# Two feed-forwards of a float32 transformer kernel: chunks 1 and 2 as seven block products instead of eight

## The reference

```python
def swiglu(x, w_gate, w_up, w_down):
    return (jax.nn.silu(x @ w_gate) * (x @ w_up)) @ w_down

x = x + 0.5 * swiglu(rmsnorm(x, g_ffn1[l]), w1_gate[l], w1_up[l], w1_down[l])
...
x = x + 0.5 * swiglu(rmsnorm(x, g_ffn2[l]), w2_gate[l], w2_up[l], w2_down[l])
```

## Time and profile before

| | |
|---|---|
| median of 3 executions | 2512.41 us (2511.56 to 2513.01) |
| profiled execution | 2513.3 us, of it the span from first to last instruction 2511.5 us |
| PE busy | 2466.2 us, 98% of the span |
| DVE busy | 1601.0 us, 64% |
| ACT, POOL busy | 892.9 us (36%), 385.6 us (15%) |
| chain that ended last | 87% PE, 9% DVE, 2% ACT |

### The profile page before, as it was taken

How to read it: one execution, slowest core, us unless ns; L and a number is a source line. 1 busy time by engine, 2 the same in 40 slices (tenths; PEclk the granted TensorE clock), 3 DMA queues, 4 the chain that set the end, 5 groups by cost and what they waited for, 6 DMA issues and landing times.

```text
span 2511.5 us, 34548 instructions
## 1 busy us (share of the span) xinstructions
PE 2466.2 (98%) x12700; PEld 2093.7 (83%) x12700; DVE 1601.0 (64%) x2548; ACT 892.9 (36%) x1406; POOL 385.6 (15%) x311
## 2 busy tenths in 40 slices
PE   8999999989999999999999999999999999999998
PEld 7888888766688888888999999888888778899997
DVE  7766666789576543488787666544217753768684
ACT  4222133368432222332332234322323652444443
POOL 2101023020121010310110102103001004211112
PEclk9999999999999999999999999999999999999999
DMA  6444435421234323323334312233232013232332
GB/s 197 145 138 151 147 96 142 101 60 42 84 117 151 94 95 97 104 73 118 110 110 129 92 57 68 86 99 93 91 109 72 22 51 101 67 118 86 117 94 75
DMA packets 372756, 250.86 MB, mean 100 GB/s; under 512 B 23248, under 2 KB 368912, under 8 KB 372624
## 3 DMA queue, kind: packets, MB, share of 16 engines
q1 hardware_dynamic: 372624, 249.10, 32.8%
HBM read 237.73 MB, written 2.10 MB: 95 GB/s over the span
## 4 chain that ended last, share of the span: by engine, by line
PE 87%; DVE 9%; ACT 2%; issue 2%; SPq 0%; POOL 0%; DMA 0%; DVEq 0%; ACTq 0%; POOLq 0%
PE PS L1151 17%; PE PS L1158 17%; PE PS L1153 17%; PE PS L1290 5%; PE PS L1292 5%; PE PS L1291 5%; PE PS L1126 3%; PE PS L1127 3%; PE PS L1129 3%; PE PS L1737 2%; DVE WL L2457 1%; PE PS L1081 1%; DVE RB L2337 1%; PE PS L1729 1%; PE PS L1540 1%
## 5 line engine op out<-in xcount | busy, mean ns | idle before, releaser
L1767 ACT ACTIVATE WH<-RAW 128x2048 fp32r<-128x2048 f32 (+2 forms) x155 | 279.4, 1803 | 389.1 <-PE PS L1158 374.8
L2274 DVE TENSOR_TENSOR WL<-RAW,WH 128x2048 fp32r<-128x2048 f32 (+3 forms) x155 | 349.4, 2254 | 87.2 <-ACT WH L1767 86.4
L1151 PE MATMUL PS<-NH,WH 128*128 128x512 f32 x1248 | 379.6, 385 | 4.6 <-DVE WL L2274 2.1
L1153 PE MATMUL PS<-NH,WL 128*128 128x512 f32 x1248 | 377.6, 384 | 0.0
L1158 PE MATMUL PS<-NL,WH 128*128 128x512 f32 x1248 | 372.6, 384 | 0.0
L1151 PEld LDWEIGHTS PS<-NH,WH 128*128 128x128 f32 x1248 | 230.6, 188 | 52.2 <-issue 5.9
L1158 PEld LDWEIGHTS PS<-NL,WH 128*128 128x128 f32 x1248 | 232.1, 188 | 47.3 <-POOL NL L3221 0.7
L1153 PEld LDWEIGHTS PS<-NH,WL 128*128 128x128 f32 x1248 | 232.1, 188 | 46.7
L3179 POOL CAST HH<-VA 128x512 f32 (+3 forms) x88 | 74.3, 844 | 1245.6 <-DVE VA L2514 585.2
L1151 PE MATMUL PS<-HH,WH 128*128 128x512 f32 (+1 forms) x828 | 237.8, 369 | 3.9 <-POOL HL L3181 2.3
L1153 PE MATMUL PS<-HH,WL 128*128 128x512 f32 (+1 forms) x828 | 237.1, 368 | 0.0
(11 more groups left out here) (436 smaller groups left out, 4568.5 us busy)
## 6 DMA issues: line engine op xcount, KB each, us to landing
RAW<-in_ffn_w_in SPq DMA_DIRECT2D x88, 512.0 KB, 4.7
MW<-in_w_mod SPq DMA_DIRECT2D x72, 512.0 KB, 3.4
RAW<-in_w_in SPq DMA_DIRECT2D x70, 512.0 KB, 3.9
RAW<-in_w_gate SPq DMA_DIRECT2D x44, 512.0 KB, 3.7
RAW<-in_w_up SPq DMA_DIRECT2D x44, 512.0 KB, 4.8
RAW<-in_w_down SPq DMA_DIRECT2D x32, 512.0 KB, 3.9
RAW<-in_ffn_w_out SPq DMA_DIRECT2D x40, 256.0 KB, 3.0
RAW<-in_w_out SPq DMA_DIRECT2D x16, 512.0 KB, 3.9
```

The lines of the kernel that those rows point to most:

```text
L1151: pe.matmul(outs[half][x], w[half][0], xh(k), start=i == 0, stop=False)
L1153: pe.matmul(outs[half][x], w[half][1], xh(k), start=False, stop=False)
L1767: act.activation(WH[1 - s][:, 0:cols], RAW[1 - s][:, 0:cols], ACT.Copy).then_inc(w_hi, 1)
L2274: dve.tensor_tensor(WL[1 - s][:, 0:cols], RAW[1 - s][:, 0:cols], WH[1 - s][:, 0:cols].bitcast(F32), ALU.subtract).then_inc(w_lo, 1)
```

## The change

In ffn1 and ffn2 the gate_up stages of chunks 1 and 2 (8 + 6 blocks each, 28 blocks in all) become seven products; chunk 0 stays as it was. The sums of input halves for them are made by DVE during chunk 0, two steps of 128 x 4 x 256 in each of its blocks 1 to 7, and four conversions by ACT. They are kept in columns of NH, NL, HH and HL that the two feed-forwards do not use. The modulation slots that stood in the gate_up stages of chunks 1 and 2 are gone from there; the slots now are, in ffn1 and in ffn2 alike, chunk 0's eight blocks and all twelve down blocks, the last down stage included. 40 slots have two vectors (42 before), ffn3 has 32 of one (30 before). `norm_c1` is applied in ffn2's last down stage. In `run_ahead`, which serves all four feed-forwards, the order of sums and low parts changes. Loops over blocks become straight code.

```diff
-BOTH = 5 * KD // 2 + 1
+BOTH = 5 * KD // 2
...
+        HLF = sb("HLF", [P, HMAX, T + TC], F32, hf)
...
+        S12 = sb("S12", [P, 2, T], F32, ff)
...
-        M0 = {"ffn1": 0, "ffn2": NF + 8, "ffn3": NF + 20}
+        M0 = {"ffn1": 0, "ffn2": BOTH, "ffn3": 2 * BOTH}
...
+        MOD_CHUNKS = [bg for bg, _ in ffn3] + [ffn1[0][0], ffn2[0][0]]
...
-            return {("ffn1", 2): 1, ("ffn2", 0): 2}.get((name, c), 0)
...
+                    n0 = plain if c == 0 else 0
...
+        SV1 = Seven("ffn1", ffn1, CHUNKS, T, CHUNKS[0], 0)
+        SV2 = Seven("ffn2", ffn2, CHUNKS, T, CHUNKS[0], SV1.u1)
+        SV3 = Seven("ffn3", ffn3, CHUNKS3, T + TC, PLAIN, SV2.u1)
+        SV4 = Seven("ffn4", ffn4, CHUNKS, T, PLAIN, SV3.u1)
+        SEVENS = (SV1, SV2, SV3, SV4)
...
+            q = 0 if i in (3, 4) else KD // 2
+            return tuple(z[:, q:q + KD // 2, T:T + TC] for z in ((NH, NLF, NL) if i in (2, 3) else (HH, HLF, HL)))
...
+            def classic_first(sv, ahead):
+
+                b0 = sv.stages[0][0]
+                for b in range(b0, b0 + sv.plain):
+                    j = b - b0
+                    if j or not (ahead or b == 0):
+                        split(b % 2, loaded(b, 1), b)
+                    act.wait_ge(pe_done, b + 1)
+                    wait(act, psum_free, after(b, -1))
+                    act.activation(SA[:, b % 2, 0:T], G[b % 2][:, :], ACT.Silu).then_inc(gate_done, 1)
+                    if j in (2, 3, 4, 6):
+                        half_high(sv, {2: 3, 3: 4, 4: 2, 6: 6}[j])
...
+            def classic_first(sv, g0, h0, m0):
+
+                b0 = sv.stages[0][0]
+                sums = halves_by_steps(sv)
+                for b in range(b0, b0 + sv.plain):
+                    j, s = b - b0, b % 2
+                    if j:
                         mods(b0, j, s, m0)
-                    if not (lead and b0 == 0):
+                    if b:
                         split(s, b)
-                    if lead:
+                    if j == 0:
                         mods(b0, j, s, m0)
-                    if low is not None:
-                        norm_low(low, j)
-                    dve.wait_ge(gate_done, j + (g0 + 1))
-                    wait(dve, h_split, after(j + h0, -1))
-                    if tok > T:
-                        dve.tensor_tensor(VA[:, s, T:tok], SA[:, s, T:tok], CU[s][:, 0:tok - T], ALU.mult)
+                    else:
+                        next(sums)
+                        next(sums)
+                    dve.wait_ge(gate_done, g0 + j + 1)
+                    wait(dve, h_split, after(h0 + j, -1))
                     dve.tensor_tensor(VA[:, s, 0:T], SA[:, s, 0:T], U[s][:, :], ALU.mult).then_inc(psum_free, 1)
                     mods_out(b0, j, s, m0)
...
             def run_ahead(b0):
 
-                for i in range(4):
-                    if i < 2:
-                        factor_sum(b0, i)
-                    elif i == 2:
-                        factor_low(b0, 0)
-                        factor_low(b0, 1)
-                        factor_sum(b0, 2)
-                        factor_sum(b0, 3)
+                factor_sum(b0, 0)
+                factor_low(b0, 0)
+                factor_low(b0, 1)
+                factor_sum(b0, 1)
                 factor_low(b0, 2)
                 factor_low(b0, 3)
+                factor_sum(b0, 2)
+                factor_sum(b0, 3)
 
...
+            def halves_by_steps(sv):
+
+                for i in (3, 4, 2):
+                    yield from half_steps(sv, i)
+                for i in (3, 4):
+                    half_lowered(sv, i)
+                    yield
+                yield from half_steps(sv, 6)
+                for i in (2, 6):
+                    half_lowered(sv, i)
+                    yield
...
+            def context_scaled(j):
+
+                for k in (2 * j, 2 * j + 1):
+                    norm_scaled(norm_c1, k)
...
+                            plain_first(bg, G0[name], h0)
                         else:
-                            plain_first(bg, G0[name], h0)
-                        b0 += PLAIN
+                            classic_first(sv, G0[name], h0, m0)
+                        b0 += sv.plain
...
+                    last = sv is SV2 and c == 2
+                    down(bd, sv.tok, by, by_ctx, True, m1, cols=kn * 2 * P, also=ctx_work if sv is SV2 and c == 0 else None,
+                         before=halves_late if sv is SV3 and c == 0 else context_scaled if last else None)
...
+                    if before is context_scaled:
+                        norm_low(norm_c1, 2 * j)
+                        norm_low(norm_c1, 2 * j + 1)
...
+                    if m is norm_x1:
+                        norm_high(norm_c1, 2 * j, 2 * j + 2)
...
-            ffn(ffn1, T, "ffn1", lambda t: 0.5)
+            ffn_sevens(SV1, "ffn1", lambda t: 0.5, None)
```

More of the change, by code:

```diff
@@ L746, in __init__ @@
                 self.u1 = u0
[L748 to L753, removed]
+        SV1 = Seven("ffn1", ffn1, CHUNKS, T, CHUNKS[0], 0)
[3 more added lines that the diff above has]
+        SEVENS = (SV1, SV2, SV3, SV4)
+        RUNS = {b: r for sv in SEVENS for b, r in sv.runs.items()}
+        for n, sv in enumerate(SEVENS):
+            t = 10 * n
+            sv.t_sum = {3: t + 4, 2: t + 8, 4: t + 12, 6: t + 16} if sv is SV4 else {3: t + 3, 4: t + 6, 2: t + 8, 6: t + 10}
+            t = 4 * n
+            sv.t_lo = {3: t + 1, 2: t + 2, 4: t + 3, 6: t + 4} if sv is SV4 else {3: t + 1, 4: t + 2, 2: t + 3, 6: t + 4}
+        W_PART = sum(kn // 2 - 1 for sv in (SV1, SV2, SV3) for kn in sv.chunks[1:])
         HALF, DSH = T // 2, RQ[:, 0:KD // 2]
         def sv_of(b):
-            return SV3 if b < ffn4[0][0] else SV4
+            return next(sv for sv in SEVENS if b < sv.stages[-1][1])
         def unit(b):
@@ L882, in pairs, with ffn @@
                     mods(b0, j, s, still_mods(m0, j) if straight else m0)
[L884 to L894, removed]
+            def ffn(sv, wg, cg, wu, cu, wd):
+                k0, m0 = 0, M0.get(sv.name)
+                for kn, (bg, bd) in zip(sv.chunks, sv.stages):
+                    with_mods = bg in MOD_CHUNKS
+                    gate_up(bg, kn, wg, cg + k0 * P, wu, cu + k0 * P, m0 if with_mods else None, True)
+                    if m0 is not None and with_mods:
+                        m0 += kn
+                    pairs(bd, KD // 2, wd, k0, kn, 0, True, m0)
+                    k0, m0 = k0 + kn, None if m0 is None else m0 + KD // 2
+            ffn(SV1, inp["w1_gate"][0], 0, inp["w1_up"][0], 0, inp["w1_down"][0])
             w_in, w_uq, w_ukv = inp["w_in"][0], inp["w_uq"][0], inp["w_ukv"][0]
@@ L1993, in out_copied @@
                                ACT.Copy).then_inc(ot_out, 1)
-            def ffn(stages, tok, m, ahead=True):
-                for c, (kn, (bg, bd)) in enumerate(zip(CHUNKS, stages)):
-                    ctx = m is norm_x1
-                    gate_up(bg, kn, tok, ahead=ahead and c == 0, high=norm_c1 if ctx and c == 1 else None)
-                    if c < 2:
-                        only_split(bd, KD // 2, ctx_work if ctx and c == 0 else None)
-                    else:
-                        split_and_square(bd, m)
             act.wait_ge(c2_s, 2)
```

185 lines of the change are left out of this document (79 added, 106 removed).

## The result

The changed kernel takes 2525.16 us (median of five executions; 2524.51 to 2525.47), the kernel before in the same comparison 2511.93; the ratio is 1.0049, 95% interval 1.0037 to 1.0062. It is slower, by some 13 us, where no measurable change was forecast. The span grew from 2511.5 to 2523.6 us.

A forecast was written before the change was run, and what follows sets the result against it. PE, busy 98% of the span, was taken as the bound where DVE keeps pace. Terms -22.5 + 5.6 + 10 + 1.5 + 3.2 = -2.2; 2513.3 - 2.2 - 0.9 gave 2510.2 us, range 2504 to 2517.

The forecast's parts named there:

- PE's work, -22.5: ffn1's and ffn2's gate_up, chunks 1 and 2: 28 blocks of 10.88 us become units of 10.08 us, -22.5 us.
- heads, +5.6: Starts of the four new runs: `mods_out` on DVE makes the first unit's `t1` 1.4 us late each, +5.6 us.
- Chunk 0, 0: Chunk 0's blocks: DVE's 3.11 us of idle covers two added half steps, some 2.3 us; cost 0.
- the slower rival: Chunk 0: half steps don't fit DVE's idle; at 2.0 us a step +12.5 us, 2522.7 us; chance 0.09.
- ffn2's last down stage, +10: DVE's load up to the last X takes 43.3 us against 33.5 set by PE: +10 us, bounds +2 and +13.
- The part without POOL's sums: ffn2's last down stage: DVE's own list of 35.9 us against PE's 33.5, 2.4 us.
- POOL's hold: ffn2's last down stage: 13.8 us of POOL work holds DVE at a share of 0.72, 9.9 us, counted as 7.4.
- The factor of three quarters: ffn2's last down stage: three quarters of DVE's list reads SBUF alone, so 9.9 us of hold became 7.4.
- The rival in which POOL hardly holds DVE: ffn2's last down stage: POOL's sums hardly delay DVE, 2.4 us instead of 10, so 2502.6 us; chance 0.28.
- The third rival: ffn2's tail and ffn3's start: PE's clock falls twice after new stalls, +4.7 us, 2514.9 us; chance 0.12.
- ffn1's last down stage, +1.5: DVE's load there, without `norm_c1` and with five POOL sums, is 32.9 us against 33.5: +1.5 us, range 0 to 3.
- `run_ahead`, +3.2: ffn3's runs: the new order makes DVE wait 0.7 us for ACT's high part of sum 1; +3.2 us, range 0 to 4.

The follow-up runs named there:

- the padded kernel: The changed kernel with Z 8 columns wider, so every tile behind Z is back at its old address; 2513.84 us, ratio to the kernel before 1.0003.

## Why the prediction was wrong

**The step that failed** is the sum of the terms: it took every stage that the change doesn't touch at its old time. The line of the diff that shrinks Z was put at nothing without a reason, in the sum and in the rivals; it costs 11.3 us in the changed kernel and 12.3 in the kernel before, by matmuls of 512 columns that cost 3% more in down stages and in the mixer. The other way round, those of 256 columns on the shifted tiles are a little shorter (117 ns for most instead of 120 from start to start), which takes off 1.3 us in the four new runs and 1.5 in ffn4's. With the tiles back in their place the kernel takes 2513.84 us, in the forecast's own range of 2504 to 2517. The mechanisms that it names were found, and their sum was 3.6 us short: ffn2's last down stage was dearer by 4.0 and ffn1's by 0.6, the heads cheaper by 0.9.

- **PE's work, -22.5**, and **heads, +5.6**. In the padded kernel the four runs are 286.9 us long, the old stages were 304.7: -17.8 against -16.9. At the four new heads PE waits 1.05 us for `t1` three times and 0.60 once, and the runs are longer than their units of 10.08 us by 1.3 three times and by 0.9, 4.7 in all, where 1.4 each was forecast. Without slots in the head a unit is 10.09 us, as forecast from ffn4. (The -33.4 that the prediction sets beside this term is a slip: 28 x 1.19 is 33.3.)
- **Chunk 0, 0.** Right: 76.99 us for its seven blocks from 28.10 on, as before the change (77.01 from 28.08). The half steps took 1.2 us each, so the slower rival, which needs 1.8, is out.
- **ffn2's last down stage, +10.** +14.0 in the padded kernel, above the upper bound of 13, +13.0 in the changed one. The part without POOL's sums was forecast at 2.4 and is 1.8, with 1.5 us in it by which the last hidden block's two POOL operations lengthen the first slot. POOL's hold was forecast at 7.4 and is these 1.5 and the sums' 9.7, 11.2 in all: the operations of the slots, which read SBUF only, were what POOL's work fell on, not three quarters of an even mix, and 3.25 us became 7.37 under four sums. The factor of three quarters is the term that was mis-sized; without it the prediction's own sum is 9.9. The rival in which POOL hardly holds DVE is wrong; the Trainium skill's rule ("SBUF — State Buffer", section "SBUF: two separate sides": an exclusive lock, the loser fully blocks) would have given 3 us more than my sum, and was nearer. Its share of 1.0 the trace doesn't show: in the last slot 4.1 us of hold go with four sums of 1.25 to 1.3 us alone, a share of 0.8.
- **The clock.** The third rival has two falls at a cost of 4.7 us. In the padded kernel both came, the first within the new wait; the second alone cost something, the 2.5 us behind the last X. In the changed kernel only the second came.
- **ffn1's last down stage, +1.5.** +2.1 in the padded kernel (41.0 us instead of 38.9), +2.6 in the changed one with its slower matmuls.
- **`run_ahead`, +3.2.** ffn3 is 3.2 us longer in the padded kernel; undoing the order brings 2.1 by the times and 3.3 by the runs of ffn3. The mechanism, the low part of sum 1 right behind the sum, costs 0.66 to 0.68 at each of three heads (0.7 forecast). That the total fits is luck in part: chunk 4's head costs nothing (0.8 forecast) and chunk 5's 1.3 (0.3 forecast).

## What to carry to other kernels

When a change alters the size of any tile in SBUF, compare the start of every matmul operand before and after, and keep moving operands and weights at the same distance modulo 512 bytes; a pad of 32 bytes was worth 11 us here. When work moves to DVE's idle time, look what POOL does in that same time, and put operations with SBUF operands where POOL rests: the same four slots cost some 12 us in a stage with POOL's sums, and 2.5 us spread over stages without.

## What the runs showed of the hardware

- A float32 matmul (fp32r operands) of 512 columns starts every 227 ns if its moving operand and its weights begin at the same place modulo 512 bytes (256 was not tried), and every 233 ns on average at a distance of 32 or 128 bytes, whichever of the two was moved (128 bytes only with the moving operand); at 64 bytes it is 229. From start to start the pattern alternates (at 128 bytes 238 and 229 ns). Those of 256 columns in the units go the other way, 120 ns at distance 0 and 116 to 120 in the medians at 32 bytes; those of 384 hardly change (173 to 175). Why was not found. It is not DVE's or ACT's work (the pace is the same while both rest); that it is a meeting of the weights' reads with the moving operand's is only a guess, and the run with HL moved alone shows that neighbours count too.
- A shift by 32 bytes of all tiles together changes nothing (ratio 1.0001).
- ffn3's down stage of chunk 4, behind the same wait of PE (2.3 us), had a stretch at a granted clock of 0.50 in nine of fifteen profiles, and was 1.2 to 1.9 us longer in these.
- Eight dependent DVE operations of 256 columns with SBUF operands took 3.0 to 3.25 us with no POOL work over them, and in the padded kernel 4.5, 5.3, 6.5 and 7.4 us with some 2.2, 2.9, 4.7 and 5.8 us of it.
